# Opening of layer 1 in a two-layer decoder trunk: order of adaLN items, row transposes and the overflow test

## The chip, the cores and the metric

The kernel runs on one core of one Trainium2 chip. The metric is device microseconds of one execution, as the median of several runs. TensorE is called PE here, VectorE DVE, ScalarE ACT, GpSimd POOL; SP (SyncE) issues all large loads.

## The reference

```python
c_act = jax.nn.silu(c)
for i in range(DEPTH):                      # DEPTH = 2
    mod = c_act @ ada_w[i] + ada_b[i]       # (1, 6*1024)
    sh_m, sc_m, g_m, sh_f, sc_f, g_f = split(mod, 6)
    h = rmsnorm(x, norm_mix_g[i]) * (1.0 + sc_m) + sh_m
    y = pool_mixer(h, ...) if i == 0 else moba_attention(h, w_qkv, w_o)
    x = x + g_m * y
    h = rmsnorm(x, norm_ffn_g[i]) * (1.0 + sc_f) + sh_f
    x = x + g_f * hier_moe(h, ...)          # 32 experts of 1024 x 256, top-1 group of 4, top-2 experts in it
return rmsnorm(x, final_norm_g)             # x: (1, 256, 1024) float32
```

All data are float32; there are 256 tokens. With 256 tokens the block attention is one causal block.

## The kernel before, in words

The five engines run programs written out by hand, which meet at semaphores; nothing is scheduled by a planner. Weights (274 MB in all) stream through a ring of four slots plus a fifth place, each of 3 MB, in the order of the SP program: SP waits until a slot's last reader has freed it (`ring_free`, `down_free`), then issues the load into it.

**Experts.** All 32 experts of a layer are run one after the other on gathered tokens, 64 token slots each. PE multiplies (`hidden_of`, `down_of`), ACT and DVE evacuate, and DVE's `put_y` (L1623 on) writes an expert's output, turned and gated, into `yT` at a place it reads from a register. The 512 slot columns are combined back onto the tokens in four blocks of 128 (`combine`, L715 on): PE turns a block of `yT` (8 transposes into banks 0 and 1), ACT and DVE copy it out, and PE adds it with 8 matmul instructions (four matmuls of 128x512, two instructions each) into banks 4 to 7. Banks 4, 5 are the halves of token tile 0; banks 6, 7 those of tile 1. The last block can only start when the last expert's output is in, that is when `dn_free` has reached E+2.

**Overflow.** An expert with over 64 tokens needs the code in `overflow`, and blocks of `combine` that could not run early are then caught up. A flag in memory (`all_early`) says whether any of that is needed. With these inputs it never is, so the tests on every engine pass over it. On PE the test stands at L752 (last block if nothing overflowed) and L754 (the overflow code with all that it contains).

**Items 8 to 15.** The product of the conditioning vector with layer 1's adaLN weights is cut into eight items of 768 columns. Item 8 is computed on DVE in eight steps (`ada_steps`, L1409 on); 9 and 10 on PE (`part`, L499 on; 32 matmul instructions of up to 512 columns, on 32 of the 128 output rows each) and are copied to memory by ACT (`take_part`). `cols` (L523 on) then turns such a row of numbers into columns with 12 matmul instructions that have one column each.

**Opening of layer 1** (L819 to L847 on PE). After the last block of `combine`, ACT squares the rows to get their sums (`tile_sums`), DVE copies them to `x_sb` (`keep_row`), a root and a reciprocal give the norm's factor, and ACT and DVE write the scaled halves of the rows to `h` (`scaled_half`, semaphores `xr_act`, `xr_dve`). PE turns these rows into columns with 16 transposes (`turn_rows`); ACT and DVE scale and shift them into `hT` (`hT_act`, `hT_dve`), for which they need the columns that `cols(8)`, `cols(9)` and `cols(10)` make (vectors `SH_M`, `SC_M`). The first projection of attention, `head_rows("q", 0, 0)`, reads `hT` and starts the long run of PE work of layer 1.

In the kernel before PE does, in this order: the last block, item 9, the first four transposes, item 10, the other twelve, then the columns of 9, 8 and 10. The transposes go to banks 0 to 3, item 9's sums to banks 2 and 3, item 10's to 4 and 5 (so `part(10)` waits until tile 0's rows have been copied out), the columns to bank 6. DVE runs steps 0 to 2 of item 8 behind the last block's evacuation, ahead of `keep_row(0, 0)`, and steps 3 to 7 behind `scaled_half(1)`.

Of the kernel before, what the change touches and what calls it, by code (L numbers as in the profile page):

```python
# [7 lines left out]
P = 128  # L8
# [103 lines left out]
def program(nc, x, c, ada_w, ada_b, norm_mix_g, norm_ffn_g, pool_w, pool_scale, w_qkv, w_o,  # L112
# [3 lines left out]
    with ctx:  # L116
# [5 lines left out]
        def S(*name):  # L122

            key = "_".join(map(str, name))
            if key not in sems:
                sems[key] = ctx.enter_context(nc.semaphore(key))
            return sems[key]
# [208 lines left out]
        def cols_at(a):  # L336

            if a in (7, 15):
                return bank[4][:, 0:NB]
            return bank[7 if a < 8 else 6][:, NB * (a % 8):NB * (a % 8 + 1)]  # L340

        bb_at = bank[3][:, 0:NL]
        strided_at = bank[7][:, 64:64 + 2 * KC]
        part_bank = [(4, 5)] * 7 + [(4, 6), None, (2, 3), (4, 5)]


        ROOTS = (0, 2, 3, 5, 6)
# [146 lines left out]
        def _(pe):  # L494
# [242 lines left out]
            def later_experts(L):  # L737

                experts(L, FRONT, STAGES[0])
                pe.wait_ge(S("pwT_ready"), 2 * (L + 1))  # L740
                for s, e in enumerate(STAGES):
                    expert_at(L, e)
                    expert_at(L, e + 1)
                    pe.wait_ge(S("dn_free", L), e + 2)
                    with pe.If(flag(pe, L, s) > 0):
                        combine(L, s)
                    for u in range(e + 2, STAGE_END[s]):
                        expert_at(L, u)
                all_early = flag(pe, L, SB - 2)
                last_results(L)  # L750
                pe.wait_ge(S("dn_free", L), E + 2)
                with pe.If(all_early > 0):  # L752
                    combine(L, SB - 1)
                with pe.If(all_early < 1):  # L754
                    overflow(L)
                    for s in range(SB - 1):
                        with pe.If(flag(pe, L, s) < 1):
                            combine(L, s)
                    combine(L, SB - 1)

            pe.wait_ge(S("cact_ready"), 1)
# [61 lines left out]
                expert_at(0, e)  # L823
            later_experts(0)

            def turn_rows(t, k0, k1):

                pe.wait_ge(S("xr_act" if k0 < 4 else "xr_dve"), t + 1)
                for k in range(k0, k1):
                    last = nc.tensor.transpose(two(0, k)[:, t * P:(t + 1) * P], h[:, t, k * P:(k + 1) * P], ident)  # L830
                    if t and k % 2:
                        last.then_inc(S("hT_full"), 1)

            part(9)
            turn_rows(0, 0, 4)
            pe.wait_ge(S("xr_dve"), 1)
            pe.wait_ge(S("x_rows"), 2)
            part(10, ready=9)
            pe.wait_ge(S("acc_act"), 2 * ADA_PE.index(10))
            turn_rows(0, 4, 8)  # L840
            turn_rows(1, 0, 4)
            turn_rows(1, 4, 8)
            pe.wait_ge(S("x_rows"), 4)
            cols(9)
            cols(8)
            pe.wait_ge(S("col_ready", 1), 1)
            cols(10)  # L847

            def place(name):

# [196 lines left out]
        def _(act):  # L1047
# [207 lines left out]
            act.wait_ge(S("col_ready", 1), 2)  # L1255
            for k in (0, 1, 4, 5):
                act.wait_ge(S("hT_full"), k // 2 + 1)
                nc.scalar.activation(hT[:, k, :], two(0, k), ACT.Identity, scale=colp[:, 1, SC_M, k:k + 1],  # L1258
                                     bias=colp[:, 1, SH_M, k:k + 1]).then_inc(S("hT_act"), 1)
            load_table(ACT.Exp)  # L1260

# [122 lines left out]
        def _(dve):  # L1384
# [286 lines left out]
            def later_experts(L):  # L1671
                experts(L, FRONT, STAGES[0])
                for s, e in enumerate(STAGES):
                    expert_at(L, e)
                    expert_at(L, e + 1)
                    with dve.If(flag(dve, L, s) > 0):
                        evac_yT(L, s)
                    for u in range(e + 2, STAGE_END[s]):
                        expert_at(L, u)
                all_early = flag(dve, L, SB - 2)  # L1680
                put_y(L, E - 2, 0)
                put_y(L, E - 1, 1)
                with dve.If(all_early > 0):
                    evac_yT(L, SB - 1)
                with dve.If(all_early < 1):
                    overflow(L)
                    for s in range(SB - 1):
                        with dve.If(flag(dve, L, s) < 1):
                            evac_yT(L, s)
                    evac_yT(L, SB - 1)  # L1690
                if L == 0:
                    ada_steps(8, 0, 3)

            def tile_sum(L, t):

# [6 lines left out]
                return bank[7][:, v * KC:(v + 1) * KC]  # L1702

            def next_columns(v):
                return bank[6][:, v * KC:(v + 1) * KC]

            for t in range(T):
                reciprocal(0, slice(t, t + 1), t + 1)
# [51 lines left out]
            keep_row(1, 1)  # L1760
            tile_sum(0, 1)
            scaled_half(1)
            ada_steps(8, 3, 8)
            dve.wait_ge(S("cols_full"), 10)
            column(1, SH_M, next_columns(SH_M))
            dve.wait_ge(S("cols_full"), 11)
            column(1, SC_M, next_columns(SC_M))
            for k in (2, 3, 6, 7):
                dve.wait_ge(S("hT_full"), k // 2 + 1)
                nc.vector.tensor_scalar(hT[:, k, :], two(0, k), colp[:, 1, SC_M, k:k + 1], colp[:, 1, SH_M, k:k + 1],  # L1770
                                        ALU.mult, ALU.add).then_inc(S("hT_dve"), 1)
            nc.vector.tensor_copy(craw[:, G_M, 0:2], next_columns(G_M)[:, 0:2]).then_inc(S("g_kept"), 1)

# [117 lines left out]
```

## Time and profile before

| | us |
|---|---|
| median of 3 runs | 787.03 (785.62 to 787.30) |
| the profiled execution | 786.15 |
| its span, first to last instruction | 784.3 |
| PE busy | 723.5 |
| DVE, ACT, POOL busy | 241.9, 170.1, 39.5 |
| mean granted PE clock | 0.972 of full speed |
| loads | 274.93 MB, mean 351 GB/s |

The profile's page gives shares of the whole span; the change touches a stretch of some 25 us (from about 341 to 366 us), so what is read below are that stretch's timelines, the chain of work that ended last, and the granted clock. Times are from the start of the span.

### The profile page before, as it was taken

The numbers are of one execution on the slowest core, as the hardware profiler recorded it, in microseconds if no ns is written. First come the engines' busy times: TensorE is split into PE (matmuls) and PEld (weight loads), VectorE is DVE, ScalarE is ACT, GpSimd is POOL, SyncE is SP. The second block draws the span as 40 slices with busy tenths as digits, with TensorE's granted clock in tenths as the row PEclk, the third lists the DMA queues.
The fourth block names the chain that finished last, engine by engine and source line by source line (L and its number), as shares of the span: only waits on it lengthen the run. The fifth ranks groups of instructions, "written<-read, shape, count | busy, mean of one in ns | idle before, by whom it ended". The sixth has DMA issues, their size and how long they took to land.

```text
span 784.3 us, 12427 instructions
## 1 busy us (share of the span) xinstructions
PE 723.5 (92%) x4568; PEld 430.2 (55%) x4568; DVE 241.9 (31%) x660; ACT 170.1 (22%) x394; POOL 39.5 (5%) x71
## 2 busy tenths in 40 slices
PE   4988699999989999979999999969999998999995
PEld 2664545555544445426888888744555554454542
DVE  0113515111211211153777553261511221121113
ACT  4112441111110111142123232244111111011113
POOL 0000000000100000000000000000000100000000
PEclk9989799999999999997999999979999999999999
DMA  8999999999999999999796755182999999999961
GB/s 342 396 400 391 412 367 377 386 418 415 420 415 417 417 416 418 403 391 331 298 378 239 237 196 232 64 333 99 386 384 422 417 417 417 416 419 414 418 246 56
DMA packets 70451, 274.93 MB, mean 351 GB/s; under 512 B 4480, under 2 KB 17920, under 8 KB 53888
## 3 DMA queue, kind: packets, MB, share of 16 engines
q1 hardware_dynamic: 70400, 274.23, 88.3%
q8 instruction: 34, 0.56, 0.3%
q14 instruction: 17, 0.14, 0.0%
HBM read 273.16 MB, written 1.05 MB: 350 GB/s over the span
## 4 chain that ended last, share of the span: by engine, by line
PE 83%; DMA 9%; DVE 3%; issue 2%; SPq 1%; ACT 1%; DVEq 0%; ACTq 0%
PE bank L496 74%; DMA ring<-in_exp_w_up_dram 5%; PE bank L616 4%; DMA ring<-in_ada_w_dram 4%; PE bank L603 2%; PE bank L726 1%; SPq L361 1%; PE bank L909 1%; DVE ye L1394 1%; PE bank L768 0%; DVE keep L1397 0%; DVE reg_h L1669 0%; DVE keep L1669 0%; DVE reg_a L1397 0%; ACT ye L1049 0%
## 5 line engine op out<-in xcount | busy, mean ns | idle before, releaser
L496 PE MATMUL bank<-ring,xe 128*64 128x256 f32 x1984 | 227.8, 382 | 6.6 <-DMA ring<-in_exp_w_up_dram 6.1
L496 PEld LDWEIGHTS bank<-ring,xe 128*64 128x64 f32 x1984 | 139.6, 137 | 78.3 <-issue 12.1
L496 PE MATMUL bank<-ring,heT 128*64 128x512 f32 x512 | 123.9, 604 | 0.0
L1394 DVE TENSOR_TENSOR reg_c<-reg_c,bank 128x128 f32<-128x128 f32 x64 | 18.5, 288 | 279.6 <-ACT reg_c L1113 279.6
L468 POOL COPY xe<-reg_a 128x512 f32 x62 | 38.1, 614 | 689.0 <-PE bank L496 368.1
L1049 ACT ACTIVATE ye<-bank 128x512 f32<-128x512 f32 (+1 forms) x72 | 41.7, 585 | 139.1 <-PE bank L496 138.9
L1113 ACT ACTIVATE reg_c<-bank 128x128 f32<-128x128 f32 x64 | 17.8, 278 | 241.1 <-PE bank L496 238.6
L496 PE MATMUL bank<-reg_b,ring 128*128 128x256 f32 x256 | 60.9, 393 | 1.7 <-ACT reg_b L1258 1.7
L1394 DVE TENSOR_TENSOR reg_b<-bank,colp 128x512 f32 x64 | 44.3, 692 | 43.3 <-issue 35.8
L496 PEld LDWEIGHTS bank<-ring,heT 128*64 128x64 f32 x512 | 31.2, 136 | 47.3 <-issue 47.0
L496 PEld LDWEIGHTS bank<-reg_b,ring 128*128 128x128 f32 x256 | 49.5, 197 | 8.9 <-issue 2.2
L496 PE MATMUL bank<-ring,cact 128*32 128x512 f32 (+1 forms) x320 | 32.8, 548 | 19.5 <-DMA ring<-in_ada_w_dram 16.9
L616 PE MATMUL bank<-cst,ye 128*128 128x128 f32 x256 | 41.9, 286 | 2.9 <-ACT ye L1049 2.9
L1397 DVE SCALAR_TENSOR_TENSOR ring<-ring,cact 128x768 f32<-128x768 f32 x42 | 42.7, 1017 | 1.2
L616 PEld LDWEIGHTS bank<-cst,ye 128*128 128x128 f32 x256 | 26.7, 140 | 28.1 <-issue 23.1
L496 PE MATMUL bank<-reg_a,ring 128*128 128x256 f32 x160 | 39.2, 405 | 2.2 <-DVE reg_a L1397 1.5
L496 PE MATMUL bank<-keep,reg_h 128*128 128x512 f32 x64 | 33.6, 691 | 4.4 <-DVE keep L1397 4.4
L603 PEld LDWEIGHTS bank<-cst,reg_c 128*128 128x128 f32 x64 | 8.9, 138 | 50.5 <-issue 48.7
L496 PEld LDWEIGHTS bank<-reg_a,ring 128*128 128x128 f32 x160 | 32.0, 204 | 8.3 <-issue 2.1
L496 PEld LDWEIGHTS bank<-ring,cact 128*32 128x32 f32 x320 | 10.3, 118 | 39.2 <-issue 38.1
L1637 DVE COPY heT<-bank 128x128 f32<-128x128 f32 x64 | 18.7, 292 | 42.3 <-PE bank L603 42.3
L496 PE MATMUL bank<-ring,reg_b 128*128 128x256 f32 x128 | 29.8, 386 | 0.0
(165 smaller groups left out, 543.5 us busy)
## 6 DMA issues: line engine op xcount, KB each, us to landing
ring<-in_exp_w_gate_dram SPq DMA_DIRECT2D x64, 1024.0 KB, 13.6
ring<-in_exp_w_up_dram SPq DMA_DIRECT2D x64, 1024.0 KB, 15.6
ring<-in_exp_w_down_dram SPq DMA_DIRECT2D x64, 1024.0 KB, 12.7
ring<-in_ada_w_dram SPq DMA_DIRECT2D x16, 1536.0 KB, 12.3
ring<-in_ada_w_dram SPq DMA_DIRECT2D x32, 768.0 KB, 12.4
ring<-in_w_qkv_dram SPq DMA_DIRECT2D x12, 1024.0 KB, 12.3
ring<-in_w_o_dram SPq DMA_DIRECT2D x4, 768.0 KB, 7.5
x_sb<-in_x_dram SPq DMA_DIRECT2D x1, 1024.0 KB, 5.1
```

The lines of the kernel that those rows point to most:

```text
L361: sp.dma_start(dst[:, a:b], src[:, a:b]).then_inc(S(name, s), 16)
L468: nc.gpsimd.tensor_copy(xe[:, b, :, :], hS[:, :, bass.ds(off, CAP)]).then_inc(S("xe_ready", L), 1)
L496: return nc.tensor.matmul(o_, l_, r_, start=start, stop=stop)
L603: return nc.tensor.transpose(dst[:, 2 * P:3 * P], he[:, b, :], ident)
L616: last = nc.tensor.transpose(dst[:, cq * P:(cq + 1) * P], ye[:, b, cq * P:(cq + 1) * P], ident)
L726: last = nc.tensor.transpose(turn_bank(s, half)[:, mq * P:(mq + 1) * P], yT[:, half * 4 + mq, s * P:(s + 1) * P], ident)
L909: last = nc.tensor.transpose(bank[5 + a][:, s * P:(s + 1) * P], sc[m % 2][a][:, s * P:(s + 1) * P], ident)
L1049: return nc.scalar.activation(o_, i_, ACT.Identity)
L1113: nc.scalar.activation(sil[:, b, :], bank[b][:, 0:P], ACT.Silu).then_inc(S("sil_ready", L), 1)
L1394: return nc.vector.tensor_tensor(o_, a_, b_, op)
L1397: return nc.vector.scalar_tensor_tensor(o_, a_, s_, b_, op0, op1)
L1637: nc.vector.tensor_copy(heT[:, b, :], bank[b][:, 2 * P:3 * P]).then_inc(S("heT_ready", L), 1)
```

## The change

On PE, for layer 0 alone, the test for overflow is moved ahead of the last block of `combine`, which then stands behind it without a test of its own; before, the block stood first and the test behind it. Items 9 and 10 follow each other at once, item 10 in banks 0 and 1. The columns now go to bank 2, and the row transposes, in four groups of four, to banks 4 to 7: the first between the columns of 9 and 8, the second between those of 8 and 10, the other two behind. On DVE, step 0 of item 8 stands ahead of the last-but-one `put_y`, steps 1 and 2 ahead of the last, step 3 behind it, steps 4 and 5 behind the evacuation of the last block, and 6 and 7 behind `scaled_half(1)`.

```diff
--- before.py
+++ after.py
@@ -337,11 +337,11 @@
 
             if a in (7, 15):
                 return bank[4][:, 0:NB]
-            return bank[7 if a < 8 else 6][:, NB * (a % 8):NB * (a % 8 + 1)]
+            return bank[7 if a < 8 else 2][:, NB * (a % 8):NB * (a % 8 + 1)]
 
         bb_at = bank[3][:, 0:NL]
         strided_at = bank[7][:, 64:64 + 2 * KC]
-        part_bank = [(4, 5)] * 7 + [(4, 6), None, (2, 3), (4, 5)]
+        part_bank = [(4, 5)] * 7 + [(4, 6), None, (2, 3), (0, 1)]
 
 
         ROOTS = (0, 2, 3, 5, 6)
@@ -749,13 +749,17 @@
                 all_early = flag(pe, L, SB - 2)
                 last_results(L)
                 pe.wait_ge(S("dn_free", L), E + 2)
-                with pe.If(all_early > 0):
-                    combine(L, SB - 1)
+                if L:
+                    with pe.If(all_early > 0):
+                        combine(L, SB - 1)
                 with pe.If(all_early < 1):
                     overflow(L)
                     for s in range(SB - 1):
                         with pe.If(flag(pe, L, s) < 1):
                             combine(L, s)
+                    if L:
+                        combine(L, SB - 1)
+                if L == 0:
                     combine(L, SB - 1)
 
             pe.wait_ge(S("cact_ready"), 1)
@@ -823,28 +827,26 @@
                 expert_at(0, e)
             later_experts(0)
 
-            def turn_rows(t, k0, k1):
-
-                pe.wait_ge(S("xr_act" if k0 < 4 else "xr_dve"), t + 1)
-                for k in range(k0, k1):
-                    last = nc.tensor.transpose(two(0, k)[:, t * P:(t + 1) * P], h[:, t, k * P:(k + 1) * P], ident)
-                    if t and k % 2:
-                        last.then_inc(S("hT_full"), 1)
+            def turn_rows(b):
+
+                for k in (2 * b, 2 * b + 1):
+                    for t in range(T):
+                        last = nc.tensor.transpose(two(4, k)[:, t * P:(t + 1) * P], h[:, t, k * P:(k + 1) * P], ident)
+                last.then_inc(S("hT_full"), 1)
 
             part(9)
-            turn_rows(0, 0, 4)
-            pe.wait_ge(S("xr_dve"), 1)
-            pe.wait_ge(S("x_rows"), 2)
             part(10, ready=9)
-            pe.wait_ge(S("acc_act"), 2 * ADA_PE.index(10))
-            turn_rows(0, 4, 8)
-            turn_rows(1, 0, 4)
-            turn_rows(1, 4, 8)
+            cols(9)
             pe.wait_ge(S("x_rows"), 4)
-            cols(9)
+            pe.wait_ge(S("xr_act"), 2)
+            pe.wait_ge(S("xr_dve"), 2)
+            turn_rows(0)
             cols(8)
+            turn_rows(1)
             pe.wait_ge(S("col_ready", 1), 1)
             cols(10)
+            turn_rows(2)
+            turn_rows(3)
 
             def place(name):
 
@@ -1255,7 +1257,7 @@
             act.wait_ge(S("col_ready", 1), 2)
             for k in (0, 1, 4, 5):
                 act.wait_ge(S("hT_full"), k // 2 + 1)
-                nc.scalar.activation(hT[:, k, :], two(0, k), ACT.Identity, scale=colp[:, 1, SC_M, k:k + 1],
+                nc.scalar.activation(hT[:, k, :], two(4, k), ACT.Identity, scale=colp[:, 1, SC_M, k:k + 1],
                                      bias=colp[:, 1, SH_M, k:k + 1]).then_inc(S("hT_act"), 1)
             load_table(ACT.Exp)
 
@@ -1678,8 +1680,14 @@
                     for u in range(e + 2, STAGE_END[s]):
                         expert_at(L, u)
                 all_early = flag(dve, L, SB - 2)
+                if L == 0:
+                    ada_steps(8, 0, 1)
                 put_y(L, E - 2, 0)
+                if L == 0:
+                    ada_steps(8, 1, 3)
                 put_y(L, E - 1, 1)
+                if L == 0:
+                    ada_steps(8, 3, 4)
                 with dve.If(all_early > 0):
                     evac_yT(L, SB - 1)
                 with dve.If(all_early < 1):
@@ -1689,7 +1697,7 @@
                             evac_yT(L, s)
                     evac_yT(L, SB - 1)
                 if L == 0:
-                    ada_steps(8, 0, 3)
+                    ada_steps(8, 4, 6)
 
             def tile_sum(L, t):
 
@@ -1702,7 +1710,7 @@
                 return bank[7][:, v * KC:(v + 1) * KC]
 
             def next_columns(v):
-                return bank[6][:, v * KC:(v + 1) * KC]
+                return bank[2][:, v * KC:(v + 1) * KC]
 
             for t in range(T):
                 reciprocal(0, slice(t, t + 1), t + 1)
@@ -1760,14 +1768,14 @@
             keep_row(1, 1)
             tile_sum(0, 1)
             scaled_half(1)
-            ada_steps(8, 3, 8)
+            ada_steps(8, 6, 8)
             dve.wait_ge(S("cols_full"), 10)
             column(1, SH_M, next_columns(SH_M))
             dve.wait_ge(S("cols_full"), 11)
             column(1, SC_M, next_columns(SC_M))
             for k in (2, 3, 6, 7):
                 dve.wait_ge(S("hT_full"), k // 2 + 1)
-                nc.vector.tensor_scalar(hT[:, k, :], two(0, k), colp[:, 1, SC_M, k:k + 1], colp[:, 1, SH_M, k:k + 1],
+                nc.vector.tensor_scalar(hT[:, k, :], two(4, k), colp[:, 1, SC_M, k:k + 1], colp[:, 1, SH_M, k:k + 1],
                                         ALU.mult, ALU.add).then_inc(S("hT_dve"), 1)
             nc.vector.tensor_copy(craw[:, G_M, 0:2], next_columns(G_M)[:, 0:2]).then_inc(S("g_kept"), 1)
 
```

PE's program at the end of layer 0 (MATMUL rows L726 are the last block's transposes, `bank<-reg_h,reg_c` its matmuls, L616 and `bank<-ring,heT` the last experts; a float32 matmul counts once here and is two matmul instructions with two weight loads in the trace, a transpose is one with one). Before:

```order
L616 MATMUL bank<-cst,ye 128x128 x4
L752 COMPARE_AND_BRANCH
L726 MATMUL bank<-cst,reg_b 128x128 x8
L496 MATMUL bank<-reg_h,reg_c 128x512 x4
L752 UNCONDITIONAL_BRANCH
L754 COMPARE_AND_BRANCH
L697 TENSOR_LOAD ov_i
L697 ISA x2
```

The same place in the changed kernel, with the end of the overflow code:

```order
L616 MATMUL bank<-cst,ye 128x128 x4
L755 COMPARE_AND_BRANCH
L697 TENSOR_LOAD ov_i
L697 ISA x2
...
L758 UNCONDITIONAL_BRANCH
L726 MATMUL bank<-cst,reg_b 128x128 x8
L496 MATMUL bank<-reg_h,reg_c 128x512 x4
L496 MATMUL bank<-ring,cact 32x512 x4
```

The branch over the overflow code (L754 before, L755 now) came behind the block; now it comes between the last expert and the block, and it carries the wait for `dn_free`.

PE's opening of layer 1, before (`bank<-ring,cact` are items 9 and 10, L830 the row transposes, the rows with 128x1 the columns, `bank<-reg_b,ring` the first projection):

```order
L830 MATMUL bank<-cst,reg_h 128x128 x4
L496 MATMUL bank<-ring,cact 32x512 x4
L496 MATMUL bank<-ring,cact 32x256 x4
L496 MATMUL bank<-ring,cact 32x512 x4
L496 MATMUL bank<-ring,cact 32x256 x4
L830 MATMUL bank<-cst,reg_h 128x128 x12
L496 MATMUL bank<-cst,ring 128x1 x6
L496 MATMUL bank<-ones,ring 128x1 x6
L496 MATMUL bank<-cst,ring 128x1 x6
L496 MATMUL bank<-reg_b,ring 128x256 x8
```

and in the changed kernel:

```order
L496 MATMUL bank<-cst,ring 128x1 x6
L834 MATMUL bank<-cst,reg_h 128x128 x4
L496 MATMUL bank<-ones,ring 128x1 x6
L834 MATMUL bank<-cst,reg_h 128x128 x4
L496 MATMUL bank<-cst,ring 128x1 x6
L834 MATMUL bank<-cst,reg_h 128x128 x8
L496 MATMUL bank<-reg_b,ring 128x256 x8
```

Sixteen transposes that stood ahead of the columns now stand among and behind them; no instruction is added or lost there. DVE's program at the same time (L1394 `reg_b<-bank,colp` is `put_y`, `ring<-ring,cact` the steps of item 8), in the changed kernel:

```order
L1417 TENSOR_SCALAR ring<-ring,cact 128x768
L1627 TENSOR_LOAD off_i
L1627 ISA x2
L1396 ISA
L1396 TENSOR_TENSOR reg_b<-bank,colp 128x8x64
L1399 SCALAR_TENSOR_TENSOR ring<-ring,cact 128x768 x2
L1627 TENSOR_LOAD off_i
L1627 ISA x2
L1396 ISA
L1396 TENSOR_TENSOR reg_b<-bank,colp 128x8x64
L1399 SCALAR_TENSOR_TENSOR ring<-ring,cact 128x768
L1691 COMPARE_AND_BRANCH
```

Before, the two `put_y` stood there with nothing between them, and the first three steps came behind the copy that follows the branch.

## Rows read from the trace of the kernel before

**Rows 1.** The page: busy time by engine.

```profile
PE 723.5 (92%) x4568; PEld 430.2 (55%) x4568; DVE 241.9 (31%) x660; ACT 170.1 (22%) x394; POOL 39.5 (5%) x71
```

**Rows 2.** Chain that ended last, 342 to 367 us: start us, us, what.

```profile
342.01 0.70 DVE reg_b L1394
342.86 1.10 PE bank L726 x8
...
344.82 3.67 PE bank L496 x8
348.49 2.66 issue
351.16 4.31 PE bank L496 x32
...
363.07 1.51 PE bank L496 x12
...
364.68 0.18 DVE colp L1394
...
365.08 1.03 ACT reg_b L1258 x2
...
366.25 6.21 PE bank L496 x16
```

**Rows 3.** PE's two branches at L754: shortest, median, longest in ns, first and last start.

```profile
L754 PEldq COMPARE_BRANCH  x2: 3558/4854/6150, 344.8 to 775.0; - x2
```

**Rows 4.** The same for PE's branches at L752.

```profile
L752 PEldq COMPARE_BRANCH  x2: 65/65/65, 342.7 to 772.8; - x2
```

**Rows 5.** DMA queues, 347 to 350.5 us: packets, MB, share.

```profile
q8 instruction: 1, 0.02, 1.9%
```

**Rows 6.** Stretches around both L754 branches: length, busy by engine, granted clock, DMA share, GB/s.

```profile
344.85:350.99 6.14, 3.64 (x8) 1.38 (x8) 5.67 (x10) 4.20 (x12) 0.00 (x0) 0.99 1.05 382
775.00:778.50 3.50, 3.50 (x8) 1.34 (x8) 0.38 (x3) 2.72 (x8) 0.00 (x0) 1.00 0.02 5
```

**Rows 7.** Stretches, PE alone: length, busy (instructions), granted clock, DMA share, GB/s.

```profile
347.50:350.80 3.30, 0.99 (x3) 1.00 1.05 367
350.90:354.20 3.30, 3.04 (x20) 0.50 1.09 348
...
364.60:371.30 6.70, 5.05 (x12) 0.50 1.07 371
...
526.50:531.70 5.20, 5.20 (x6) 0.50 0.99 418
```

**Rows 8.** PE in order of time: start us, us, line, operation, count.

```profile
355.99 2.79 PE L496 MATMUL bank<-ring,cact 128*32 128x512 f32 x32
358.70 1.53 PE L830 MATMUL bank<-cst,reg_h 128*128 128x128 f32 x12
360.07 1.40 PE L496 MATMUL bank<-cst,ring 128*128 128x1 f32 x12
...
373.17 3.62 PE L496 MATMUL bank<-reg_b,ring 128*128 128x256 f32 x16
```

**Rows 9.** ACT in order of time.

```profile
351.91 0.69 ACT L1244 ACTIVATE reg_h<-bank,rs 128x512 f32<-128x512 f32 x1 [0.23 <-DVE rs L1428]
355.10 0.97 ACT L1049 ACTIVATE ring<-bank 128x512 f32<-128x512 f32 x2 [2.50 <-PE bank L496]
```

**Rows 10.** DVE in order of time.

```profile
338.84 0.69 DVE L1394 TENSOR_TENSOR reg_b<-bank,colp 128x512 f32 x1 [1.13 <-PE bank L616]
342.01 0.69 DVE L1394 TENSOR_TENSOR reg_b<-bank,colp 128x512 f32 x1 [2.48 <-PE bank L616]
...
345.44 2.07 DVE L1397 SCALAR_TENSOR_TENSOR ring<-ring,cact 128x768 f32<-128x768 f32 x2
...
352.58 5.22 DVE L1397 SCALAR_TENSOR_TENSOR ring<-ring,cact 128x768 f32<-128x768 f32 x5
```

**Rows 11.** Who ended the waits of SP's queue, 300 to 784 us: us, times, longest.

```profile
SPq L388 <- ACTq L1123: 156.5, 30, 11.3
```

## Prediction

> **What bounds the kernel now.** The page comes first: PE is busy 723.5 of 784.3 us [rows 1], the other engines far less, so what leaves PE idle or slow counts. The second view is the chain of work that ended last, between 342 and 367 us [rows 2]. It runs from the last expert's `put_y` (342.01) over the block's transposes (342.86) to its eight matmul instructions, which end at 348.49. Then PE stands for 2.66 us on "issue", a wait for which the chain names no partner. Item 9 follows at 351.16, and after item 10, the transposes and the columns, the first projection starts at 366.25. So 17.76 us lie between the end of the block and the projection. The reader is to see that this stretch has almost no other work to hide behind: whatever it gains or loses goes to the start of the long attention run.
>
> The third view gives the source line of PE's branches, and explains the 2.66 us. The branch over the overflow code (L754) took 6.150 us in one layer and 3.558 in the other [rows 3], where the branch next to it took 65 ns [rows 4]. It began at 344.8, while its eight matmuls were queued, and covered itself with them: 344.84 + 6.15 = 350.99, and item 9 starts at 351.16. It skips some 300 instructions. In this time the DMA queue for instructions brings one packet of 0.02 MB, in the stretch from 347 to 350.5 [rows 5]: PE waits for code. The loads keep the DMA engines full in this stretch (share 1.05), and nearly empty at the other branch (0.02), which took 3.558 us [rows 6]. **So a jump over this code costs 6.15 us beside full loads, 3.56 without, and 3.5 of the 6.15 are hidden today.**
>
> **The branch, moved ahead of the block.** In the changed program the jump stands between `put_y` and the block, with the wait for `dn_free` on it, so it can't begin before 342.74 (the time at which L752 begins now, [rows 4]). Queued behind it on PE is the whole block, and ACT and DVE wait for that. Nothing is left to cover it. Its price in this place isn't in the trace; the bounds are 0.07 us (a branch whose target is at hand, [rows 4]) and 6.15 us. I take 6.15: it is the same code that is skipped, two microseconds earlier, beside the same loads. The transposes then start at 348.95 in place of 342.86, **6.1 us later**.
>
> **The clock.** PE is then idle from about 342 to 349 us. In the kernel before, a stretch with 0.99 us of work in 3.30 was followed by one at granted clock 0.50 [rows 7], that is 1.2 GHz in place of 2.4. Seven idle microseconds will do the same, so I expect the block at 0.50. It came back after 3.04, 5.05 and 5.20 us of work at the lower level [rows 7]; I take 5.1, the two that agree, and keep 3.0 and the whole block as ends. At the lower level a matmul row takes double: 16 rows of 128x256 took 6.21 us at 366.25 and 3.62 at 373.17 [rows 2, 8], with the clock returning within the first. From the first transpose to the first matmul lie 1.96 us now (342.86 to 344.82); four more transposes at half speed ahead of each copy add 0.8, so the matmuls start at 348.95 + 2.75 = 351.7. At full speed they come every 0.43 us (3.67 for eight, with the last one's tail). Six at 0.86 take 5.1 us, to 356.8; two at 0.43 and a tail of 0.15 end at **357.8, which is 9.3 us later** than 348.49. Ends: with 3.0 us at the lower level 356.8, with all eight at it 358.7.
>
> **Behind the block.** (1) Items 9 and 10 follow without the stand of 2.66 us and, the clock having returned, at 2.79 us each (item 10 now, [rows 8]; item 9 took 4.31 at 0.50): 5.5 us. (2) That the columns of 9 start then needs its copy by ACT. ACT's scaled half of tile 1 starts 3.42 us behind the block's end (351.91) and takes 0.69, the copy 0.97 [rows 9], together 5.1 us. It is just in time. (3) Columns of 9, four transposes, columns of 8, four transposes: 1.3 + 0.45 + 1.3 + 0.45 = 3.5 us, from 12 column rows in 1.40 and 12 transposes in 1.53 [rows 8]. Steps 6 and 7 of item 8 end about 4.2 + 2.1 = 6.3 us behind the block (five steps take 5.22, [rows 10]), ahead of the columns of 8 at 7.25. (4) From the start of the columns of 10 (363.07) to the projection (366.25) lie 3.18 us [rows 2], through DVE's vector and ACT's first two pieces of `hT`; the last eight transposes stand in the shadow of that. Sum: 5.5 + 3.5 + 3.2 = 12.2 us in place of 17.76, **5.55 us won**. The copies go to and from other banks than before, and item 10 no longer waits for tile 0's copies; neither is late in the trace, so I price this at nothing.
>
> **Item 8's steps.** DVE was idle 1.13 and 2.48 us ahead of the two last `put_y` [rows 10]. Step 0 (0.62 us) goes into the first gap, steps 1 and 2 (2.07 us) into the second, step 3 behind `put_y`, where DVE now waits over six microseconds for PE. Their cover is DVE's idleness; were step 2 late, `put_y` would be too, at most 0.4 us. Two steps in place of three ahead of `keep_row(0, 0)` win 0.6 us for tile 0's root; tile 1 sets the end, so I take nothing. SP can issue the second projection's weights only when item 8 is finished, some 6.5 us later than now; its reader stands behind the first projections, of which two rows alone take 6.21 and 3.62 us [rows 2, 8], so I price this at nothing too.
>
> **The sum.** The projection starts at 357.8 + 12.2 = 370.0 in place of 366.25: **+3.75 us**. It starts at the lower clock in both kernels (364.6 to 371.3 at 0.50, [rows 7]), behind the stretch of one-column matmuls and waits, which is 6.7 us long now and was 7.5; that term cancels. From there on PE is without gaps until the experts, where SP's loads wait for slots that are freed behind PE (156.5 us of waits for ACT's frees, [rows 11]); a late start shifts them alike. Against the profiled execution of 786.15 us that is 789.9; the median of the runs lies 0.88 above that execution, so the forecast is 790.8.
>
> **Rivals.** *The target is at hand* (faster). If the jump is short by then, the block ends at 348.5, the clock doesn't fall, and the 5.55 us are won: 787.03 - 5.55 = 781.5. It decides if what follows the skipped code is already in PE's instruction store when the branch begins; from a price of some 2.4 us on (5.55 less 3.2 that the lower clock costs) nothing would be left. For it: the skipped code is shorter by one block, eight transposes and four matmuls. Against: both L754 branches paid [rows 3], and one instruction packet came only behind the branch [rows 5]. The Trainium skill (Runtime: NRT & Kernel Launch, "Instruction fetch mechanics") gives PE room for 2048 instructions, by which some 300 would be a jump inside what is held; the same section says that a taken branch outside a window of two pages makes a DMA fetch, and that is what the measured 6.150 us look like. 1 in 10.
>
> *The jump at the price of an idle DMA.* If the fetch finds the queues quieter, it costs 3.56 us [rows 3, 6]: transposes at 346.4, matmuls from 349.1, six at the lower level to 354.3, end at 355.2, projection at 367.4: +1.1 us, 788.2. Prices between lie between. Against it: from 344.85 on the DMA engines are full [rows 6]. 1 in 10, together with the case next.
>
> *The clock stays up.* Then the block ends at 354.6, the projection starts at 366.8: +0.55 us, 787.6. The rows at 0.50 behind shorter idleness speak against it [rows 7].
>
> *The change doesn't do what it says*: the tests might be passed over in another order. The program's order shows the branch ahead of the block, so this has no share.
>
> **How the numbers follow.** What a measurement of this kernel can tell from no change is about 0.2%, 1.6 us. The main case (full price, lower clock) has 8 in 10; its ends are 789.8 (3.0 us at the lower level) and 791.7 (the whole block at it), and with 0.8 us for the scatter of runs 789 to 792.5. The cheaper jump and the clock that stays up take the range down to 787.6; 0.7 us more are added on top for a jump that costs more beside fuller loads. The faster case is left out of the range. Slower by over 0.2% (above 788.6): 0.8; within 0.2%: 0.09, from the second and third rival; faster: 0.11.
>
> **What would show it.** In the changed kernel's trace: the branch at L755 starts at 342.7 with some 6.15 us, and the page of waits puts six microseconds of "issue" ahead of the L726 transposes; granted clock 0.50 from before 351 until about 357; the block ends near 357.8; items 9 and 10 in one piece of some 5.5 us; the projection near 370. The forecast is wrong if L755 takes under 3 us, if the clock stays at 1.00 through the block, or if the first projection starts before 367 us.

## The result and the profile of the changed kernel

| | before | changed |
|---|---|---|
| median of the runs, us | 786.77 (783.25 to 788.58, 7 runs) | 791.68 (788.40 to 793.53, 7 runs) |
| profiled execution, span | 786.15, 784.3 | 788.40, 786.6 |
| mean granted PE clock | 0.972 | 0.965 |

The ratio is 1.0063 with a 95% interval of 1.0036 to 1.0090: slower by 4.9 us, against a forecast of 3.75 over the profiled execution.

The page of the changed kernel, busy time by engine, which answers to [rows 1]:

```profile
PE 725.2 (92%) x4568; PEld 433.3 (55%) x4568; DVE 241.8 (31%) x660; ACT 169.8 (22%) x394; POOL 39.5 (5%) x71
```

PE has as many instructions as before, and they are busy 1.7 us longer. The change is read from the chain that ended last, over the same piece of program as [rows 2]:

```profile
339.24 0.70 DVE reg_b L1396
339.94 6.18 issue
346.12 1.98 PE bank L726 x8
...
348.13 0.70 DVE reg_h L1671
...
348.96 12.54 PE bank L496 x84
361.50 0.50 PE bank L834 x4
362.00 1.24 PE bank L496 x12
363.24 0.57 PE bank L834 x4
363.81 2.40 PE bank L496 x12
366.21 1.81 PE bank L834 x8
368.02 4.77 PE bank L496 x16
```

Six microseconds of "issue" now stand between the last `put_y` (L1396) and the block's transposes (L726); they stood beside the block before. The "issue" of 2.66 us behind the block is gone. The branches, one in each layer, as [rows 3]:

```profile
L755 PEldq COMPARE_BRANCH  x2: 331/3212/6094, 340.0 to 777.2; - x2
```

In layer 0 the branch takes 6.094 us, from the moment `put_y` has ended. In layer 1 it takes 0.331 us, where the same test cost 3.558 before, though nothing was edited there. The forecast had not expected that.

PE in order of time, and the granted clock of the same stretches (length, PE busy with instructions, clock, DMA share, GB/s):

```profile
346.12 1.97 PE L726 MATMUL bank<-cst,reg_b 128*128 128x128 f32 x8 [7.02 <-issue]
348.96 5.81 PE L496 MATMUL bank<-reg_h,reg_c 128*128 128x512 f32 x8 [0.87 <-DVE reg_h L1671]
354.71 5.37 PE L496 MATMUL bank<-ring,cact 128*32 128x512 f32 x64
360.00 1.50 PE L496 MATMUL bank<-cst,ring 128*128 128x1 f32 x12
...
363.61 2.61 PE L496 MATMUL bank<-cst,ring 128*128 128x1 f32 x12
366.07 1.95 PE L834 MATMUL bank<-cst,reg_h 128*128 128x128 f32 x8
367.89 4.90 PE L496 MATMUL bank<-reg_b,ring 128*128 128x256 f32 x16
```

```profile
342.80:348.90 6.10, 1.97 (x8) 0.52 1.05 375
347.50:350.80 3.30, 2.43 (x5) 0.50 1.09 349
350.90:354.20 3.30, 3.30 (x7) 0.64 1.09 349
354.30:357.60 3.30, 3.30 (x38) 1.00 0.27 88
...
364.50:367.90 3.40, 3.40 (x18) 0.50 1.09 351
```

The clock was at 0.50 of 2.4 GHz, that is 1.2 GHz, when the transposes began, and came back within the block, which took 5.81 us in place of 3.67.

The two profiled executions differ in what came before this stretch: layer 0 reached the last `put_y`'s end at 342.70 before and at 339.93 here, which nothing in the change explains (the clock fell at other places in the first 100 us). So the comparison is made from that point. **From the last `put_y` to the first projection: 23.55 us before, 27.96 in the changed kernel, 4.4 us more. From the projection to the end: 418.1 and 418.7.** Of the loss in these two executions 4.4 us lie in the opening and 0.7 behind it.

### The profile page after: what moved, and what is told of

It reads as the page before. It is cut to its first block, busy times and chain, and to the rows that moved or that the text cites. A ratio compares the mean times of both kernels' runs of the same rounds, so it can differ in the third digit from the quotient of the medians.

```text
span 786.6 us, 12424 instructions
## 1 busy us (share of the span) xinstructions
PE 725.2 (92%) x4568; PEld 433.3 (55%) x4568; DVE 241.8 (31%) x660; ACT 169.8 (22%) x394; POOL 39.5 (5%) x71
## 4 chain that ended last, share of the span: by engine, by line
PE 82%; DMA 9%; DVE 3%; issue 2%; SPq 1%; ACT 1%; DVEq 0%; ACTq 0%
PE bank L496 73%; DMA ring<-in_exp_w_up_dram 5%; PE bank L616 4%; DMA ring<-in_ada_w_dram 4%; PE bank L603 2%; PE bank L726 1%; SPq L361 1%; PE bank L911 1%; DVE ye L1396 1%; DVE keep L1399 0%; PE bank L772 0%; PE bank L834 0%; DVE reg_h L1671 0%; DVE keep L1671 0%; DVE reg_a L1399 0%
## 5 line engine op out<-in xcount | busy, mean ns | idle before, releaser
L1396 DVE TENSOR_TENSOR reg_c<-reg_c,bank 128x128 f32<-128x128 f32 x64 | 18.4, 288 | 278.7 <-ACT reg_c L1115 278.7
L1396 DVE TENSOR_TENSOR reg_b<-bank,colp 128x512 f32 x64 | 44.3, 692 | 40.2 <-issue 36.0
L616 PE MATMUL bank<-cst,ye 128*128 128x128 f32 x256 | 42.0, 287 | 2.9 <-ACT ye L1051 2.9
L496 PE MATMUL bank<-ring,cact 128*32 128x512 f32 (+1 forms) x320 | 30.9, 525 | 14.3 <-DMA ring<-in_ada_w_dram 14.3
L616 PEld LDWEIGHTS bank<-cst,ye 128*128 128x128 f32 x256 | 26.7, 140 | 28.1 <-issue 23.1
## 6 DMA issues: line engine op xcount, KB each, us to landing
ring<-in_ada_w_dram SPq DMA_DIRECT2D x16, 1536.0 KB, 13.1
```

The source lines that it names most:

```text
L496: return nc.tensor.matmul(o_, l_, r_, start=start, stop=stop)
L616: last = nc.tensor.transpose(dst[:, cq * P:(cq + 1) * P], ye[:, b, cq * P:(cq + 1) * P], ident)
L1396: return nc.vector.tensor_tensor(o_, a_, b_, op)
```

## The experiments

All times of a stretch are read from one profiled execution each. "To projection" is from the end of the last `put_y` to the first projection; "to probabilities" goes on to the first transposes of the attention probabilities (L909 before, L911 in the changed kernel). The runs of the kernel before had medians of 786.3, 787.2 and 788.1 us in the three groups (e1 to e4, e5 to e8, e9 and e10); the ratios are against the runs of the same group.

| | median us (runs) | ratio, 95% interval | branch, layer 0 / 1 | to projection | to probabilities |
|---|---|---|---|---|---|
| before | | | 6.150 / 3.558 | 23.55 | 54.2 |
| changed | 791.68 (7) | 1.0063, 1.0036 to 1.0090 | 6.094 / 0.331 | 27.96 | 57.8 |
| e1 test behind | 784.15 (10) | 0.9976, 0.9945 to 1.0007 | 6.174 / 3.382 | 21.92 | 51.4 |
| e2 +112 instructions | 786.33 (10) | 1.0002, 0.9969 to 1.0035 | 0.457 / 3.742 | 21.73 | 51.5 |
| e3 +256 instructions | 803.97 (4) | 1.0225, 1.0180 to 1.0271 | 6.229 / 0.331 | 28.16 | 58.1 |
| e4 filler beside branch | 787.76 (10) | 1.0020, 0.9990 to 1.0050 | 4.562 / 0.331 | 22.79 | 53.9 |
| e5 branch alone | 792.63 (10) | 1.0091, 1.0064 to 1.0118 | 6.074 / 0.331 | 30.68 | 61.2 |
| e6 shorter skip | 784.52 (12) | 0.9976, 0.9949 to 1.0003 | 0.369 / 3.538 | 21.28 | 50.8 |
| e7 behind, +112 | 787.35 (12) | 1.0005, 0.9977 to 1.0033 | 0.362 / 0.452 | 18.31 | 53.2 |
| e8 before, +112 | 788.55 (12) | 1.0019, 0.9980 to 1.0058 | 0.362 / 3.518 | 22.17 | 54.5 |
| e9 e7, DVE reordered | 785.20 (12) | 0.9967, 0.9945 to 0.9988 | 0.462 / 3.327 | 21.18 | 51.1 |
| e10 e1, DVE reordered | 784.46 (12) | 0.9971, 0.9947 to 0.9996 | 5.823 / 3.297 | 21.86 | 50.7 |

### The branch against the rest of the change (e1, e5)

e1 is the changed kernel with PE's test put back behind the block; e5 is the kernel before with that test alone moved ahead. For e1:

```diff
-                if L:
-                    with pe.If(all_early > 0):
-                        combine(L, SB - 1)
+                with pe.If(all_early > 0):
+                    combine(L, SB - 1)
                 with pe.If(all_early < 1):
                     overflow(L)
...
-                    if L:
-                        combine(L, SB - 1)
-                if L == 0:
                     combine(L, SB - 1)
```

> The whole change but for the overflow test on PE, which stands behind the last block again. Theory (the jump over the overflow code costs some 6.1 us and the change took its cover away, the rest of the change wins): the branch takes about 6.1 us from the start of the block's matmuls, stands in PE's way for 2.7 us behind them, the block runs at granted clock 1.00, and from the end of the last put_y to the first projection it is some 20.6 us (before 23.5, changed kernel 28.0). Time 3 us under the kernel before. Rival (the new order of items, columns and transposes is what costs): the stretch stays at 26 us or more and the time at 790 or above.

> The kernel before with only PE's overflow test of layer 0 moved ahead of the last block; order of columns and transposes, banks and item 8's steps as before. If the moved branch carries the whole loss: it takes 6.1 us with nothing beside it, the block runs at the lower clock and ends 14.8 us behind the last put_y as in the changed kernel, and behind it the old order needs 17.76 - 2.66 (the stand that is gone) - 1.5 (item 9 at the full clock) = 13.6 us, so last put_y to first projection 28.5 us, 0.5 more than the changed kernel and 4.9 more than before; median near 791.5. Rival, that the new order of columns and transposes costs the time: 23.5 us and the median of before. Layer 1's branch: its target lies in the next block of 256 instructions as in the changed kernel, 0.33 us.

e1's PE in order of time:

```profile
339.70 1.08 PE L726 MATMUL bank<-cst,reg_b 128*128 128x128 f32 x8 [0.99 <-DVE reg_b L1392]
341.66 3.67 PE L496 MATMUL bank<-reg_h,reg_c 128*128 128x512 f32 x8 [0.88 <-DVE reg_h L1667]
348.04 5.37 PE L496 MATMUL bank<-ring,cact 128*32 128x512 f32 x64 [2.71 <-issue]
...
361.46 4.63 PE L496 MATMUL bank<-reg_b,ring 128*128 128x256 f32 x16
```

And e5's:

```profile
349.51 1.97 PE L726 MATMUL bank<-cst,reg_b 128*128 128x128 f32 x8 [7.00 <-issue]
352.36 6.65 PE L496 MATMUL bank<-reg_h,reg_c 128*128 128x512 f32 x8 [0.88 <-DVE reg_h L1673]
358.94 2.79 PE L496 MATMUL bank<-ring,cact 128*32 128x512 f32 x32
```

With the test behind, PE waits 0.99 us for `put_y`, the block takes 3.67 us, and the stand of 2.71 us is back. With the test ahead, in the old order too, PE stands 7.00 us on issue and the block takes 6.65. The four kernels form a square: to the probabilities, the branch adds 7.0 us in the old order (61.2 - 54.2) and 6.4 in the new one (57.8 - 51.4); the new order wins 2.8 us with the test behind and 3.4 with it ahead. By this, in one execution of each, one part of the change won 3 us and the other lost 6 to 7. The whole times say the same in direction: e5 is 0.9% over before, the changed kernel 0.6% over, and e1 0.2% under, with an interval that just takes in no change. e5 came out 2.2 us over the 28.5 expected: 0.8 in the block and 1.2 in the columns of 10, which ran at the lower clock (2.72 us, against 1.51 in [rows 2]). In e1 too the clock had fallen ahead of the projection (0.50 from 356.5 on), so the stretch to it took 21.92 us and not the 20.6 expected.

### What the branch pays for (e2, e3, e6)

The price of 6.09 us may come from the number of instructions skipped, or from where the target lies. e2 and e3 put 28 and 64 one-column matmuls at the start of PE's program, of four instructions each in the way this program is laid out (a float32 matmul is two matmul instructions and two weight loads): 112 and 256 instructions.

```diff
+            pe.wait_ge(S("ones_ready"), 1)
+            for _ in range(28):
+                mm(bank[3][:, 0:1], ones[:, :], ones[:, 0:1], True, True)
             pe.wait_ge(S("cact_ready"), 1)
             part(0)
```

> The changed kernel with 28 one-column matmuls (112 PE instructions) ahead of PE's first work, while PE waits for its first load anyway. Theory (what the jump costs is set by where PE's code is cut into fetched pieces: the trace shows one instruction packet of 16 KB about every 256 instructions, and in the changed kernel one only 3.6 us behind the branch): the shift puts the jump's target into the piece that is already there, the branch takes under 0.4 us, the block runs at full clock, put_y to projection is some 18 us, and the time is 5 us under the kernel before. Rival (the cost goes with the number of instructions skipped, or with any taken branch forwards): the branch still takes 6 us and the time stays near 791.7.

> The changed kernel with 64 one-column matmuls (256 PE instructions) at the same place: the control. Theory of the pieces of 256 instructions: the cuts fall where they fell, so the branch takes 6.1 us again, put_y to projection 28 us, time as the changed kernel (+4.5 us on before). Rival (extra matmuls at the start or a shift of any size help): as with 112.

e6 leaves layer 0's overflow code out of PE's program:

```diff
                 with pe.If(all_early < 1):
-                    overflow(L)
+                    if L:
+                        overflow(L)
```

> The changed kernel with the overflow code of layer 0 (172 instructions of PE that are never run here) left out of PE's program, so that the same branch jumps over 130 instructions in place of 298. If the price hangs on whether the target lies in the block of 256 instructions that is already fetched: L755 takes under 0.5 us in layer 0, and 3.4 to 3.8 us in layer 1, where nothing but the place of the code changes; last put_y to projection 18 to 22 us (22 where the granted clock falls ahead of the block), median 784 to 787. Rival, that any taken branch here pays the fetch: 6.1 us, 28 us, median as the changed kernel.

The branch in e2, e3 and e6, in this order, each from its own kernel (shortest, median, longest in ns):

```profile
L755 PEldq COMPARE_BRANCH  x2: 457/2100/3742, 340.4 to 771.4; - x2
```
```profile
L755 PEldq COMPARE_BRANCH  x2: 331/3280/6229, 351.3 to 788.1; - x2
```
```profile
L755 PEldq COMPARE_BRANCH  x2: 369/1954/3538, 340.1 to 772.1; - x2
```

The same jump over the same code cost 6.094, 0.457 and 6.229 us with 0, 112 and 256 instructions ahead of it. **In layer 0 what it costs hangs on where the code lies relative to a period of 256 instructions (or a divisor of it that doesn't go into 112), and not on how much it skips.** Layer 1 says the same in these kernels: 3.558 us before, 0.331 in the changed kernel, 3.742 with 112 more, 0.331 again with 256 more. e6 moves the target nearer and lowers layer 0's price to 0.369, while layer 1's, whose code only slid by some 170 instructions (by the counts in the expectation), rose to 3.538. The DMA queue for instructions brings packets of 0.02 MB. In the changed kernel one of them comes between 342.8 and 346 us, behind the branch and just ahead of the transposes it releases:

```profile
q8 instruction: 1, 0.02, 2.1%
```

The Trainium skill (Runtime: NRT & Kernel Launch, "Instruction fetch mechanics") says that code arrives in 16 KiB blocks of 256 instructions, one ahead of the one that runs, and that a taken branch to a target outside the window of two must fetch first. The prices with 0, 112 and 256 instructions agree with that; that the target lay outside the window where the jump paid is a count of the program, which no trace shows, and a pair of kernels at the end of this text does not fit. The figure of the same section for PE's room, 2048 instructions, does not help here: the jump over 298 instructions (the count in e6's expectation) took 6.094 us.

Most of e3's 17 us is the padding itself: it keeps PE busy until 28.5 us, where the changed kernel's first work starts at 10.25, and the first expert starts at 126.0 us in place of 114.4. It is a control for the branch, not for the time. The shorter padding isn't free either: in e2, e7 and e8 it ends at 13.2 us, so PE's first work starts at 13.1; the first expert of e2 and e7 starts at 115.3 and 115.5, against 113.9 to 114.4 in the changed kernel, e1, e6 and e10.

e2 took 21.73 us to the projection and not 18, since the clock fell at the block though the stall was gone: the eight matmul instructions took 6.32 us. Its median is that of before, where 5 us less were expected. The clock in the block:

```profile
344.00:349.40 5.40, 5.40 (x12) 0.59 1.05 371
```

### How much of the loss is the clock (e4)

e4 is the changed kernel with twelve 512-column matmul instructions on constants between the last expert and the branch. They write a bank that is free then, and nobody reads the result.

```diff
+                if L == 0:
+                    for _ in range(6):
+                        mm(bank[2][:, :], ident, iota, True, True)
                 if L:
                     with pe.If(all_early > 0):
```

> The changed kernel with six full-width float32 matmuls of constants (12 matmul rows of 128x512, about 5 us) into bank 2, ahead of the overflow branch of layer 0; what they compute is not used. Theory (about 2.3 us of the loss in the block, and 0.8 in its transposes, is the lower granted clock that follows the idle jump): the branch takes 6.1 us as before, but the clock stays at 1.00, transposes 1.1 and matmuls 3.7 us, put_y to projection some 25 us, time 3 us under the changed kernel. Rival (the clock falls anyway, or the block waits for something else): matmuls 5.8 us or more and the time as the changed kernel's.

```profile
342.86 5.42 PE L496 MATMUL bank<-cst 128*128 128x512 f32 x12 [0.89 <-DVE reg_b L1399]
348.11 1.04 PE L726 MATMUL bank<-cst,reg_b 128*128 128x128 f32 x8
350.02 3.67 PE L496 MATMUL bank<-reg_h,reg_c 128*128 128x512 f32 x8 [0.88 <-DVE reg_h L1674]
```

The transposes start 5.3 us behind `put_y` in place of 6.2, at the full clock, and the block ends at 10.9 in place of 14.84. So 3.1 us of the changed kernel's loss at the block were the clock: 0.93 in the transposes (1.97 against 1.04), 2.14 in the matmuls (5.81 against 3.67). The columns of 10 stayed at the full clock as well, and the projection started at 22.79 us, 5.2 earlier than in the changed kernel. Filling the wait with useless work thus gave back the loss; the median, 787.76, can't be told from the kernel before. The filler also moved the code by 24 instructions and the branch took 4.562 us in place of 6.094, so not all of the 5.2 us is the clock; in the block itself it is read from the durations, and in all three kernels with the full stall (changed, e3, e5) the transposes took 1.97.

### A better version, and the wait behind it (e7 to e10)

e7 joins both remedies: e1 with e2's padding. e8 is the kernel before with that padding alone.

> Both remedies: the test behind the block as in the first experiment, and 28 one-column matmuls (112 instructions of PE) at the start. The branch's target then lies in the next block of instructions, requested some 90 instructions earlier: L754 under 0.5 us in layer 0, no stand of 2.7 us between block and item 9, last put_y to projection 21.9 - 2.7 = 19.2 us, 4.3 less than before; median 782 to 784. If the stand has another cause than code: 21.9 us, 784.

> The kernel before with the same 112 instructions of padding at the start and nothing else. If the 2.66 us on issue behind the block are the fetch of the branch's target: L754 under 0.5 us in layer 0, last put_y to projection 23.55 - 2.66 = 20.9 us, or 19.4 where item 9 then runs at the full clock; median 1 to 3 us under before. Rival: the padding matters only through the start of the kernel, 23.5 us.

The stand behind the block was the branch: with 0.362 us for it, item 9 follows the block at once in both. The new order reaches the projection in 18.31 us, 5.2 less than before. e8 took 22.17 and not 20.9, since its block ran at the lower clock (6.04 us for the eight matmul instructions), and its median is not under before's. Nor is e7's. The chain of waits shows where the first part of e7's gain went. Its PE and DVE in order of time (376.92 are the scores of the first two heads):

```profile
376.92 0.93 PE L496 MATMUL bank<-reg_a 64*128 64x128 f32 x8
...
382.28 3.72 PE L496 MATMUL bank<-ring,reg_b 128*128 128x256 f32 x16
389.98 5.18 PE L496 MATMUL bank<-reg_b,ring 128*128 128x256 f32 x16 [3.98 <-ACT reg_b L1050]
```
```profile
376.79 0.62 DVE L1416 TENSOR_SCALAR ring<-ring,cact 128x768 f32<-128x768 f32 x1 [10.15 <-DMA ring<-in_ada_w_dram]
...
379.58 6.28 DVE L1398 SCALAR_TENSOR_TENSOR ring<-ring,cact 128x768 f32<-128x768 f32 x6
386.12 0.61 DVE L1398 SCALAR_TENSOR_TENSOR reg_c<-cst,bank 128x384 f32<-128x384 f32 x1 [0.26 <-DVE ring L1398]
```

The scores of the first two heads, which DVE's `front(0)` reads, are there at 377.85 (376.92 + 0.93). But `front(0)` stands behind the eight steps of item 11, whose weights landed at 376.6, and starts at 386.12. Behind it ACT takes the exponentials and only then copies out a block of values, and PE, which needs that copy's bank, waits 3.98 us until 389.98. In e1 `front(0)` started at 383.51, and PE waited 0.15 us. e9 puts three of the steps behind `front(0)`; e10 does the same to e1, as a control.

```diff
-            ada_steps(11, 2, 8)
+            ada_steps(11, 2, 5)
             front(0)
+            ada_steps(11, 5, 8)
```

> The seventh experiment's kernel with DVE's steps 5 to 7 of item 11 moved behind front(0). In the seventh, the projection started 18.31 us after the last put_y and the first L910 transposes 34.89 us later, 53.2 us together, since front(0) stood behind item 11's eight steps, whose weights landed at 376.6. If that order is the wait that took the gain: front(0) starts when the scores are there (PE's 382.35 in that profile, in place of 386.12), PE's wait of 3.98 us ahead of the L496 matmuls falls under 0.6, and last put_y to L910 is 49.5 us, 1.8 less than in the first experiment and 4.7 less than before; median 782 to 785. If something else holds PE there (weights, ACT), 53 us.

> Control: the first experiment's kernel (test behind the block, no padding) with the same reordering of DVE. There DVE reached front(0) at 383.51 and the scores were there at 383.57, so nothing should be won: last put_y to L910 51.3 us as in the first experiment, PE's wait at that place under 0.3; median 783 to 786. Its branch pays 6.1 us behind the block, with the stand of 2.7 us. If the reordering helps by itself: under 50 us.

The two expectations name the wrong moment for the scores. 382.35 in e7 and 383.57 in e1 are the ends of the second group of eight matmul instructions, the scores of heads 2 and 3, which `front(1)` reads. Those for `front(0)` were there 4.5 us earlier, in e1 too (at 379.06), so in neither kernel was `front(0)` held by its scores. What met in e1 was PE and ACT's copy.

e9's PE at the block and at the place of the wait, and its DVE:

```profile
348.44 6.49 PE L496 MATMUL bank<-reg_h,reg_c 128*128 128x512 f32 x8 [0.88 <-DVE reg_h L1670]
...
385.02 0.93 PE L496 MATMUL bank<-reg_a 64*128 64x128 f32 x8
...
390.39 3.72 PE L496 MATMUL bank<-ring,reg_b 128*128 128x256 f32 x16
393.94 3.62 PE L496 MATMUL bank<-reg_b,ring 128*128 128x256 f32 x16
```
```profile
383.82 3.12 DVE L1398 SCALAR_TENSOR_TENSOR ring<-ring,cact 128x768 f32<-128x768 f32 x3
386.85 0.61 DVE L1398 SCALAR_TENSOR_TENSOR reg_c<-cst,bank 128x384 f32<-128x384 f32 x1
```

The wait of 3.98 us is gone: `front(0)` starts at 386.85, where the old order would have held it to about 390.1 (383.82 and the 6.28 us that e7's six steps took), with the scores there at 385.95. But that is hardly the reordering's work. In e7 PE went on 3.9 us after `front(0)` had begun. From 390.1, or 390.4 with e7's gap of 0.26 us, that would be about 394.2 in e9, and PE came there at 393.94 anyhow, since its own projection had started 2.9 us later behind `put_y` than e7's. So the old order would have cost e9 some 0.3 us by this estimate. That DVE's order made the wait is read from e7's chain (e8, in the old order too, waited 1.17 us there); what the reordering gives a kernel as early as e7 was not measured. In e10 `front(0)` started at 380.33, 3.2 us earlier than in e1, and only the 0.15 us could go.

A gain in the whole time from the reordering is not shown either: e9's median is 785.20 us and its ratio 0.9967, against 1.0005 for e7, but the two are from different groups and their intervals overlap (0.9945 to 0.9988, 0.9977 to 1.0033). The stretch came to 51.1 us against the 49.5 expected; the clock, which fell through the block, alone cost 2.8 there (6.49 against 3.67). e10 took 50.7, near the 51.3 expected, and its ratio is 0.9971, against 0.9976 for e1. e1, e6, e9 and e10 all lie 0.2 to 0.3% under before, and e9 and e10 have intervals clear of 1, e10's by 0.0004. **The version to keep is e10 or e1: the new order, with the test behind the block as before.** A gain of some 2 us over before is likely by these four together; that the padding or the reordering adds anything is not shown.

## Why the prediction came out right

"The branch, moved ahead of the block" held to a tenth: 6.094 us against 6.15, transposes 6.19 us behind `put_y` against 6.2. The reasoning had a gap, though. It took the price as that of a jump over this code, whichever its place, and that the price carried over was luck. The rival "the target is at hand" named the right condition, whether what follows the skipped code is already there, but was weighed by how long that code is. With 112 instructions more at the start, as in e2, it came true: 0.457 us for the jump, a median of 786.33, and a forecast of slower would have been wrong. By a count of the program, which no trace shows, the moved test has its target two blocks ahead in layer 0, and that would be why it paid in full; in layer 1 the same reasoning would have missed by 3.2 us (0.331 against 3.558), which didn't matter beside the last block. That full loads make the difference between 6.15 and 3.56 us was read from one layer against the other; the other kernels repeat it (5.8 to 6.2 in layer 0, 3.3 to 3.7 in layer 1), but no run changed the loads at one branch.

"The clock" held: block's end 14.84 us behind `put_y`, forecast 15.1; e4 shows that it was the clock that made the block 3.1 us longer. "The clock stays up" fell with it for this kernel, and in e3 and e5 the clock fell behind the seven idle microseconds too. But its fall behind short idleness, which the forecast held against that rival, is not certain: behind the same 0.99 us the block ran at full clock in e1 and e7 and mostly at half in e8 and e9.

"Behind the block" forecast 12.2 us, and 13.2 were measured (354.71 to 367.89). Term (1) gave 5.3 for 5.5 and term (3) 3.6 for 3.5. Term (4), from the columns of 10 to the projection, was undersized: 4.28 us in place of 3.18. The clock fell at 363.5 already, so the columns of 10 took 2.61 us, where the forecast let it fall only for the projection. Of the 5.55 us forecast as won, 2.66 are the stand, which the branch took along to its new place. Of the other 2.9, e1 shows 1.6 at the projection (21.92 against 23.55, its clock having fallen) and 2.8 by the probabilities.

"Item 8's steps" cost nothing, as forecast. DVE was there for the last `put_y`, and waited 7.27 us for the block's transposes behind them:

```profile
339.24 0.69 DVE L1396 TENSOR_TENSOR reg_b<-bank,colp 128x512 f32 x1 [0.27 <-PE bank L616]
339.85 1.01 DVE L1399 SCALAR_TENSOR_TENSOR ring<-ring,cact 128x768 f32<-128x768 f32 x1
348.13 0.69 DVE L1671 COPY reg_h<-bank 128x512 f32<-128x512 f32 x1 [7.27 <-PE bank L726]
```

"The sum" said +3.75 us at the projection, +4.4 were measured, by term (4). That what follows shifts alike held here (418.1 and 418.7), and that too was in part luck: from the projection to the end it is 418.0 us in e5, but 419.9 to 424.8 in the other nine. One piece of that is the last block of layer 1, whose eight matmul instructions took 3.67 us in the kernel before, the changed one and e5, and 5.37 to 6.51 in those nine, again by the clock (2.5 us more in e1). Nor would it have held for a gain: in e7 the 3.6 us won beyond e1 at the projection, and 1.8 more, were lost before the probabilities (53.2 against 51.4). The forecast named no such wait for the faster rival and gave it the full 5.55 us.

Open: the rest of the difference between the stretch (4.4 us) and the medians (4.9) is within their scatter. The padded kernels have medians 0.7 to 1.8 us above unpadded ones with a like stretch (e2 against e6, e9 against e10). The padding's own late start, about 1 us at the first expert, is of that size, but that it is the cause was not tried.

## What to carry to other kernels

A test whose code never runs isn't free: ask what runs beside it, and put it behind queued work rather than ahead of it. A branch's price depends on where the compiled code happens to lie, so a change far ahead of it, here of 112 instructions, can add or remove 3 to 6 us. A price read from one program may not hold in a changed one; vary the place of the code, as e2 does, before trusting it. When a stall is taken away, look for the next in-order queue, here DVE's adaLN steps ahead of the first scores.

## What was not expected of the hardware

The same taken branch cost, mostly by its offset, 0.36 to 0.46 or 5.8 to 6.2 us in layer 0, and 0.33 to 0.45 or 3.3 to 3.7 us in layer 1; 4.56 us in e4, where the filler stood ahead of it. Nothing between these levels was seen in the other runs.

One pair doesn't fit. e7 and e9 have the same PE program, and paid 0.452 and 3.327 us in layer 1. In e7 an instruction packet had come between 764 and 768 us, ahead of the branch, here first; in e9 none came from 755 until one between 776 and 780, second:

```profile
q8 instruction: 1, 0.02, 1.7%
```
```profile
q8 instruction: 1, 0.02, 1.5%
```

Only DVE's program differs between the two. What moved the edge is open.

The clock also fell in unlike places of like programs: the block took 3.67 us at 2.4 GHz in the kernel before, e1, e4, e7 and e10 and 5.37 to 6.49 in e2, e6, e8 and e9, with 0.99 to 1.39 us of idleness ahead of its transposes in all but e4. This scatter of 2 to 3 us at one place is as large as most of the effects here, and may be why medians of ten runs still have intervals of 0.3%.
